# A hybrid decoder block on one core: the mixer in natural channel order, and a first and last expert pass with loads in halves

## The chip, the cores and the metric

The program runs on one core of one Trainium2 chip. The metric is the device time of one execution in microseconds, the median of several runs; lower is better. Everything is float32.

## What is computed

One decoder block over 256 tokens of 1024 channels: a pooling branch and a sliding-window attention branch, both gated, an output projection with a residual, then a top-4-of-32 mixture of experts with a residual, and a last RMSNorm. Cut to what matters here:

```python
h = rmsnorm(x, norm1_g)
u, q, k, v, g_pool, g_attn = split(h @ w_in)              # w_in 1024 x 3328
mixed = sigmoid(g_pool) * y_pool + sigmoid(g_attn) * y_attn
x = x + mixed @ w_out                                     # w_out 1024 x 1024
t = rmsnorm(x, norm2_g)
gates = softmax over the 4 largest of t @ w_router + b_router, 0 elsewhere
for e in range(32):                                       # w_up 1024 x 2048, w_down 1024 x 1024 each
    out += gates[:, e] * (clamped_swiglu(t @ w_up[e] + b_up[e]) @ w_down[e] + b_down[e])
return rmsnorm(x + out, final_g)
```

The experts' weights are 403 MB of the 430 MB that the program moves.

## The kernel before

**Ring of weights.** All large weights go through `ring`, ten slots of 2 MB (16 KB in each of the 128 partitions). SyncE (SP) issues the loads in one fixed order: 11 for the mixer, then 12 for each of 16 passes. A pass handles two experts, up to 64 chosen tokens of each. Its loads 0 to 7 are `w_up` in four steps `kk` of two experts each (two k rows to a slot, a k row being 128 of the 1024 input channels), loads 8 to 11 are `w_down` in two steps. `wait_freed` makes SP wait, before it issues a load, until TensorE is done with the load that lay in the same slot: semaphore `up_done` for `kk` 0 to 2, `cols_done` for `kk` 3, `down_done` for the two down steps. In pass 0, loads 0 to 9 wait for units of the mixer (`last_use`), load 8 for `w_out0_done`, load 9 for `outT3`; loads 10 and 11 wait for `kk` 0 of pass 0 itself (L309 issues them), and loads 0 and 1 of pass 1 for its `kk` 1.

**Mixer.** x is turned on TensorE (L592), normalized by DVE into `hT` (L981), and multiplied with the columns of `w_in` (L612, L623, L632). A channel of the model lies in partition p as k of `(p k)`, so the turned x and the output projection take every eighth column: `acc[:, t, k:D:KD]` at L592 and `w[:, k % 4, c:D:KD]` in `out_part` (L716). `out_part(c, k)` writes channel group c of the new x, turned; DVE adds the old x (L1082) into `x1T`. For each c TensorE then runs `logits_part`: the router's matmuls (L731), and sums of squares as matmuls of the ACT's squares (L511) with a column of ones (L735). `turn_back` (L742) turns `x1T` back; ACT and DVE copy it twice, scaled into `x1r` (L520) and plain into `acc` (L523, L1187).

**Routing and passes.** ACT takes the root (L513), DVE computes logits, the four chosen experts and ranks (L1087 to L1113) around three small matmuls (L770 to L772), and builds the 0/1 matrix `pick`. `gather` (L782) fetches a pass's tokens out of `x1r`, DVE copies them to `xgT` with the norm's weight (L1139). `pe_pass` runs the `up` matmuls (L827, 16 for each `kk`; TensorE takes each as two instructions), then `turn_hid` (L820) turns each half of the activated result for the `down` matmuls (L878), and four matmuls (L914) scatter the result back; DVE adds them to `acc` (L1144). The activation of chunk j of four is DVE's L1168, L1169, L1171, the ACT's sigmoid L547, DVE's product L1174, on one set of buffers. Pass 0 also holds `up_bias`, a second gather, two turns and `down_bias`.

**The end.** In pass 15 the last two loads are split by columns into six smaller ones (L318, semaphores `tail_landed`). ACT squares `acc` in four pieces of 512 columns (L567), takes two roots (L573), DVE scales and stores are issued by SP in three pieces (L1255, L382, L385).

Queues: SP issues all weights and the stores, ACT's queue the small inputs, POOL's queue two transfers of the attention bias. Each engine runs its own instructions in the order of the program.

```python
ins = nc.tensor.matmul(...)                 # up, kk < 3: all j for k, then the next k
ins.then_inc(up_done, 1)                    # once per kk
for j in range(NJ):                         # kk == 3: both k for j, then the next j
    for k in (2 * kk, 2 * kk + 1):
        ins = up(k, j, w)
    ins.then_inc(cols_done, 1)
```

## Time and profile before

| what | value |
|---|---|
| median of 3 runs | 1114.65 us (1114.25, 1114.65, 1119.39) |
| the profiled execution, its own time | 1119.8 us |
| its span, first to last instruction | 1118.0 us |
| TensorE (PE) busy | 1033.2 us, 92% |
| DVE, ACT, POOL busy | 250.0, 104.9, 8.3 us |
| DMA | 429.99 MB, 385 GB/s over the span |
| mean granted TensorE clock | 0.978 of full speed |

The profile's page gives busy times of each engine (PEld is TensorE's weight load, beside its matmuls), the span in 40 slices, the chain of waits that ended last, groups of instructions by line and tile, and the DMA issues. A matmul's busy time is partly modelled, so the distance between starts says more than the duration of one. SPq and ACTq rows are DMA issues of those engines.

### The profile page before, as it was taken

The page shows a single profiled execution, that of the slowest core. Times are in us where ns is not written, and L with a number is a line of the kernel's source. Part 1 is how long each engine was busy: PE and PEld are TensorE (multiplying, and loading weights), DVE is VectorE, ACT ScalarE, POOL GpSimd, SP SyncE. Part 2 cuts the span into 40 slices and gives each one's busy share as a digit, 9 for nine tenths or more (in the row PEclk, how much of TensorE's full clock was granted, in tenths as well). Part 3 has the DMA queues.
Part 4 walks back from the last instruction along what each step waited for, and adds up shares of the span by engine and source line. Part 5 has one row for each costly group of instructions (what it writes and reads, how often), then busy time and mean ns, then how long its engine had stood idle before and what let it go on. Part 6 is the DMA issues. An engine that isn't in the chain of part 4 may idle for free.

```text
span 1118.0 us, 11365 instructions
## 1 busy us (share of the span) xinstructions
PE 1033.2 (92%) x4930; PEld 504.1 (45%) x4930; DVE 250.0 (22%) x562; ACT 104.9 (9%) x238; POOL 8.3 (1%) x20
## 2 busy tenths in 40 slices
PE   7999998999999998989898989898989899898987
PEld 6888897343333434333333424242424243333322
DVE  2332113322121212121212213030212121212122
ACT  2131013000000000000000000010100000000002
POOL 1100000000000000000000000000000000000000
PEclk9999998999999999999999999999999999999998
DMA  9703982899999999999999999999999999999993
GB/s 335 293 1 136 427 376 81 357 429 427 427 429 427 426 429 427 427 429 426 428 429 427 428 429 428 427 428 427 428 428 427 428 426 429 427 427 429 428 414 135
DMA packets 42367, 429.99 MB, mean 385 GB/s; under 512 B 4771, under 2 KB 6604, under 8 KB 17996
## 3 DMA queue, kind: packets, MB, share of 16 engines
q1 hardware_dynamic: 39952, 427.57, 91.0%
q0 software_dynamic: 304, 1.06, 0.3%
q10 hardware_dynamic: 2060, 0.61, 0.3%
q8 instruction: 41, 0.67, 0.2%
q14 instruction: 10, 0.08, 0.0%
HBM read 428.16 MB, written 1.06 MB: 384 GB/s over the span
## 4 chain that ended last, share of the span: by engine, by line
PE 54%; DMA 44%; issue 0%; SPq 0%; DVE 0%; ACT 0%; DVEq 0%; ACTq 0%
DMA ring<-in_w_down 39%; PE bank L827 17%; PE bank L878 14%; PE bank L612 9%; PE bank L914 4%; DMA ring<-in_w_up 4%; PE bank L716 3%; PE bank L782 2%; PE bank L623 1%; PE bank L811 1%; DMA ring<-in_w_in 1%; PE bank L820 1%; SPq L309 0%; PE bank L632 0%; PE bank L735 0%
## 5 line engine op out<-in xcount | busy, mean ns | idle before, releaser
L827 PE MATMUL bank<-ring,z_buf 128*64 128x512 f32 x2048 | 468.8, 612 | 50.0 <-issue 27.7
L827 PEld LDWEIGHTS bank<-ring,z_buf 128*64 128x64 f32 x2048 | 156.7, 141 | 347.2 <-issue 347.2
L878 PE MATMUL bank<-ring,h_buf 128*64 128x512 f32 x1024 | 228.5, 598 | 10.6 <-DMA ring<-in_w_down 10.0
L878 PEld LDWEIGHTS bank<-ring,h_buf 128*64 128x64 f32 x1024 | 80.4, 137 | 136.0 <-issue 133.9
L1168 DVE TENSOR_SCALAR swi<-bank 128x256 f32<-128x256 f32 x64 | 27.2, 425 | 310.0 <-PE bank L827 304.9
L612 PE MATMUL bank<-h_buf,ring 128*128 128x256 f32 x336 | 75.7, 380 | 0.0
L612 PEld LDWEIGHTS bank<-h_buf,ring 128*128 128x128 f32 x336 | 63.5, 190 | 8.8 <-issue 0.2
L782 PE MATMUL bank<-u_buf,m_buf 128*128 128x128 f32 x512 | 63.5, 278 | 0.5 <-DVE u_buf L1123 0.5
L547 ACT ACTIVATE swi<-swi 128x256 f32<-128x256 f32 x64 | 26.7, 417 | 387.1 <-DVE swi L1168 387.1
L782 PEld LDWEIGHTS bank<-u_buf,m_buf 128*128 128x128 f32 x512 | 60.9, 195 | 1.3 <-issue 1.3
L914 PE MATMUL bank<-y,u_buf 128*128 128x512 f32 x128 | 59.2, 605 | 0.0
L1139 DVE TENSOR_TENSOR z_buf<-bank,g2x 128x512 f32<-128x512 f32 x32 | 22.1, 692 | 158.6 <-PE bank L782 158.6
L1144 DVE TENSOR_TENSOR acc<-acc,bank 128x512 f32<-128x512 f32 x64 | 44.0, 687 | 30.1 <-PE bank L914 30.1
L914 PEld LDWEIGHTS bank<-y,u_buf 128*128 128x128 f32 x128 | 23.0, 189 | 35.2 <-issue 35.2
L1179 DVE COPY y<-bank 128x512 f32<-128x512 f32 x16 | 11.1, 692 | 116.1 <-PE bank L878 116.1
L716 PE MATMUL bank<-m_buf,ring 128*128 128x256 f32 x128 | 32.8, 411 | 0.0
L538 ACT COPY h_buf<-bank 128x512 f32<-128x512 f32 x32 | 18.5, 577 | 145.9 <-PE bank L820 145.9
L716 PEld LDWEIGHTS bank<-m_buf,ring 128*128 128x128 f32 x128 | 31.1, 335 | 0.0
L820 PEld LDWEIGHTS bank<-ident,h_buf 128*128 128x128 f32 x128 | 17.8, 209 | 26.0 <-issue 26.0
L534 ACT COPY u_buf<-bank 128x256 f32<-128x256 f32 x16 | 6.0, 373 | 242.8 <-PE bank L790 242.8
L1174 DVE TENSOR_TENSOR h_buf<-swi 128x256 f32<-128x256 f32 x64 | 27.2, 425 | 2.5
L1171 DVE SCALAR_TENSOR_TENSOR swi<-swi 128x256 f32<-128x256 f32 x64 | 27.2, 425 | 2.2
(176 smaller groups left out, 374.0 us busy)
## 6 DMA issues: line engine op xcount, KB each, us to landing
ring<-in_w_up SPq DMA_DIRECT2D x128, 2048.0 KB, 36.8
ring<-in_w_down SPq DMA_DIRECT2D x62, 2048.0 KB, 36.8
ring<-in_w_in SPq DMA_DIRECT2D x6, 2048.0 KB, 18.3
ring<-in_w_out SPq DMA_DIRECT2D x2, 2048.0 KB, 16.5
ring<-in_w_pool_proj SPq DMA_DIRECT2D x1, 2048.0 KB, 24.5
ring<-in_w_attn_proj SPq DMA_DIRECT2D x1, 2048.0 KB, 22.3
ring<-in_w_down SPq DMA_DIRECT2D x2, 1024.0 KB, 32.1
ring<-in_w_down SPq DMA_DIRECT2D x4, 512.0 KB, 11.0
```

Of the source, the lines that this page charges most:

```text
L547: nc.scalar.activation(sig, glu, ACT.Sigmoid, scale=ALPHA).then_inc(sigmoid_ready, 1)
L612: ins = nc.tensor.matmul(dst, w[:, k, c * P:(c + 1) * P], rhs[:, k, :], start=(k == 0), stop=(k == kn - 1))
L716: return nc.tensor.matmul(outs[c % 4][:, (c // 4) * SEQ:(c // 4 + 1) * SEQ], w[:, k % 4, c:D:KD], mixedT[:, k, :], start=(k == 0 and c < 4 ...
L782: ins = nc.tensor.matmul(b[:, k * P:(k + 1) * P], x1r[:, t, (4 * half + k) * P:(4 * half + k + 1) * P], pick[:, t, :], start=(t == 0), sto ...
L820: ins = nc.tensor.transpose(turn_bank[:, c * P:(c + 1) * P], hid[:, m * CH + c:(m + 1) * CH:4], ident[:, :])
L827: ins = nc.tensor.matmul(up_banks[j][e * SLOTS:(e + 1) * SLOTS, :], xgT[:, k, e * SLOTS:(e + 1) * SLOTS], w[e].rearrange("p (k n) -> p k n ...
L878: ins = nc.tensor.matmul(down_banks[n][e * SLOTS:(e + 1) * SLOTS, :], hidT[:, k, e * SLOTS:(e + 1) * SLOTS], w[e], start=(k == 0), stop=(k ...
L914: nc.tensor.matmul(scatter_banks[q][:, :], spreadT[:, t * P:(t + 1) * P], y[:, n * CH:(n + 1) * CH], start=True, stop=True).then_inc(scatt ...
L1144: nc.vector.tensor_tensor(acc[:, t, n * CH:(n + 1) * CH], acc[:, t, n * CH:(n + 1) * CH], scatter_banks[q][:, :], ALU.add).then_inc(added, 1)
L1168: nc.vector.tensor_scalar(glu, pairs[:, :, 0], LIMIT, None, ALU.min).then_inc(glu_ready, 1)
L1171: nc.vector.scalar_tensor_tensor(lin, lin, 1.0, glu, ALU.add, ALU.mult).then_inc(gated_ready, 1)
L1174: nc.vector.tensor_tensor(hid[:, j * CF:(j + 1) * CF], lin, sig, ALU.mult).then_inc(hid_ready, 1)
```

## The change

In words:

- **Channel order.** `w_in`, `w_router` and the norm weights are loaded with `(k p)` instead of `(p k)`, so channel k * 128 + p lies in partition p. The transposes of x (L592) and the weights of `out_part` (L716) become contiguous. `norm1_g` in that order is a load of 1024 single elements; so is a second load of `norm2_g` (`g2`); `w_router` becomes 1024 pieces of 128 B. The experts keep `(p k)`; `turn_back` is now a matmul with a permuted identity (`deal`) instead of a transpose, and ACT's copy writes `x1r` in the experts' order.
- **Squares.** DVE adds the squares of groups 0 to 6 into `sq_sum`; TensorE sums only `sq_sum` and the last group, in a bank of its own and ahead of the last logits.
- **Copies to `acc`.** The plain copies of ACT and DVE (L523, L1187) are gone; POOL writes `acc` from `x1r` and `std`.
- **`keep_warm`.** Matmuls of the identity whose result is not used: 7 before the ranks, 2 before and 3 behind the first gather, 4 and 5 in the last pass.
- **First pass.** Loads 10 and 11 come in halves: the first when k row 0 of `kk` 0 is done (`rows_freed`), the second when row 1 is done.
- **Last pass.** Loads 6 to 9 come in halves with semaphores of their own; `kk` 3 runs k row by k row; both `turn_hid` stand ahead of the down matmuls; the activation uses two sets of buffers, and POOL does the product; two scatter matmuls stand between the last down matmuls, and the copy of the second half of `y` and its two scatters go in halves of 256 columns (the copy in every pass).
- **The end.** POOL multiplies columns 0 to 511 with `final_g`, ACT scales and stores them; DVE does columns 512 to 1023, which SP stores.

```diff
-                             w_in_d[:, c * CH:c * CH + wide].rearrange("(p k) n -> p k n", p=P)).then_inc(full[n % R], LANDED)
+                             w_in_d[:, c * CH:c * CH + wide].rearrange("(k p) n -> p k n", p=P)).then_inc(full[n % R], LANDED)
...
+                if g == FIRST:
+                    for h in range(2):
+                        sp.wait_ge((rows_freed, up_done)[h], 1)
+                        for load in (LOADS - 2, LOADS - 1):
+                            load_half(slot_of(load), g, load, h, early_landed[h])
+                if g == LAST:
+                    for load, landed in ((UP_LOADS - 2, last_up_landed), (UP_LOADS, last_down_landed)):
+                        for e in range(2):
+                            wait_freed(g, load + e)
+                        for h in range(2):
+                            for e in range(2):
+                                load_half(slot_of(g * LOADS + load + e), g, load + e, h, landed[h])
...
+            for t in range(TT):
+                pool.wait_ge(*emptied_at("back3"))
+                nc.gpsimd.tensor_scalar(acc[:, t, :].rearrange("p (q k) -> p k q", k=KD), x1r[:, t, :].rearrange("p (k q) -> p k q", k=KD),
+                                        std[:, t:t + 1], None, ALU.mult).then_inc(x1_ready, 1)
+            for j in range(NJ):
+                glu, lin, sig = gate_bufs(j, True)
+                pool.wait_ge(gated_ready, LAST * NJ + (j + 1))
+                pool.wait_ge(sigmoid_ready, LAST * NJ + (j + 1))
+                nc.gpsimd.tensor_tensor(hid[:, j * CF:(j + 1) * CF], lin, sig, ALU.mult).then_inc(hid_ready, 1)
...
-            act.dma_start(g1x, norm1_g[0].rearrange("(p k) -> p k", p=P)).then_inc(g1x_loaded, 16)
+            act.dma_start(g1, norm1_g[0].rearrange("(k p) -> p k", p=P), allow_slow_non_contiguous=True).then_inc(g1_loaded, 16)
...
+            for t in range(TT):
+                act.wait_ge(rstd_ready, 2 * TT + t + 1)
+                act.wait_ge(scaled_ready, t + 1)
+                nc.scalar.activation(result[:, t, 0:CH], result[:, t, 0:CH], ACT.Copy, scale=rstd[:, t:t + 1]).then_inc(result0_ready, 1)
...
-                return nc.tensor.matmul(outs[c % 4][:, (c // 4) * SEQ:(c // 4 + 1) * SEQ], w[:, k % 4, c:D:KD], mixedT[:, k, :],
+                return nc.tensor.matmul(outs[c % 4][:, (c // 4) * SEQ:(c // 4 + 1) * SEQ], w[:, k % 4, c * P:(c + 1) * P], mixedT[:, k, :],
...
+            def squares_part(src, first):
+                for t in range(TT):
+                    ins = nc.tensor.matmul(square_bank[:, t:t + 1], src[:, t, :], ones[:, 0:1],
+                                           start=(first and t == 0), stop=not first, skip_group_check=True)
+                return ins
...
+            def keep_warm(b, n):
+                for _ in range(n):
+                    nc.tensor.matmul(b[:, 0:P], ident[:, :], ident[:, :], start=True, stop=True)
...
+                            if first and kk == 0:
+                                ins.then_inc((rows_freed, up_done)[k], 1)
...
+                    elif split:
+                        for k in (2 * kk, 2 * kk + 1):
+                            pe.wait_ge(last_up_landed[k % 2], 32)
+                            for j in range(NJ):
+                                ins = up(k, j, w)
+                                if k == KD - 1:
+                                    ins.then_inc(cols_done, 1)
```

TensorE between the mixer's last group and the first pass, as it stood (L731 router, L735 squares, L742 turns back, L770 ranks, L782 gather, L827 pass 0):

```order
L731 MATMUL bank<-rt_buf,h_buf 128x32 [waits x1T_ready]
L731 MATMUL bank<-rt_buf,h_buf 128x32
L735 MATMUL bank<-row_buf,swi 128x1 [waits x1sq_ready]
L735 MATMUL bank<-row_buf,swi 128x1
L742 MATMUL bank<-ident,h_buf 128x128
L742 MATMUL bank<-ident,h_buf 128x128 [waits emptied_by_dve]
L770 MATMUL bank<-swi,row_buf 128x32 [waits x1T_ready,chosen_ready,consts]
L782 MATMUL bank<-u_buf,m_buf 128x128 [waits pick_ready,x1r_ready]
L782 MATMUL bank<-u_buf,m_buf 128x128 x7
```

and as it stands now (L804 router, L810 squares, L817 turns back, L824 `keep_warm`, L856 ranks, L868 gather):

```order
L810 MATMUL bank<-row_buf,swi 128x1 [waits x1sq_added,emptied_by_dve]
L817 MATMUL bank<-u_buf,h_buf 128x128 [waits deal_ready]
L810 MATMUL bank<-row_buf,swi 128x1 [waits x1sq_ready]
L804 MATMUL bank<-rt_buf,h_buf 128x32 [waits x1T_ready]
L804 MATMUL bank<-rt_buf,h_buf 128x32
L817 MATMUL bank<-u_buf,h_buf 128x128 x2
L824 MATMUL bank<-ident 128x128 [waits x1T_ready]
L824 MATMUL bank<-ident 128x128 x6
L856 MATMUL bank<-swi,row_buf 128x32 [waits x1T_ready,chosen_ready,consts]
L868 MATMUL bank<-u_buf,m_buf 128x128 [waits pick_ready]
```

The squares moved ahead of the last logits, and seven unused matmuls stand between the turns and the ranks.

SP's loads of the first pass after the mixer's, now (before, the four L341 rows were one row of two L309 loads that waited for `up_done`):

```order
L329 DMA ring<-in_w_down 128x4096 [waits unit_done]
L341 DMA ring<-in_w_down 128x2048 [waits rows_freed]
L341 DMA ring<-in_w_down 128x2048
L341 DMA ring<-in_w_down 128x2048 [waits up_done]
L341 DMA ring<-in_w_down 128x2048
L325 DMA ring<-in_w_up 128x4096 [waits up_done] x4
```

The first half moved ahead of the second k row; the loads of pass 1 behind them wait for what they waited for.

TensorE in the last pass, now (L913 up, L906 turns, L982 down, L1010 scatter):

```order
L913 MATMUL bank<-ring,z_buf 64x512 [waits last_up0_landed]
L913 MATMUL bank<-ring,z_buf 64x512 [waits last_up1_landed]
L906 MATMUL bank<-ident,h_buf 128x128 [waits hid_ready]
L824 MATMUL bank<-ident 128x128 x5
L906 MATMUL bank<-ident,h_buf 128x128 [waits hidT_copied,hid_ready]
L982 MATMUL bank<-ring,h_buf 64x512 [waits last_down0_landed,hidT_copied,spreadT_copied]
L982 MATMUL bank<-ring,h_buf 64x512 [waits tail1_landed]
L1010 MATMUL bank<-y,u_buf 128x512 [waits y0_copied]
L982 MATMUL bank<-ring,h_buf 64x512 [waits tail2_landed]
L1010 MATMUL bank<-y,u_buf 128x256 [waits y1_copied] x2
L1010 MATMUL bank<-y,u_buf 128x256 x2
```

The second turn moved ahead of the down matmuls, and two scatters ahead of the last of them.

## Rows read from the trace of the kernel before

**Rows 1.** Page, part 2: GB/s of the DMA in 40 slices of 27.95 us.
```profile
GB/s 335 293 1 136 427 376 81 357 429 427 427 429 427 426 429 427 427 429 426 428 429 427 428 429 428 427 428 427 428 428 427 428 426 429 427 427 429 428 414 135
```

**Rows 2.** Windows: PE, PEld, DVE, ACT, POOL busy us; PEclk, DMA share, GB/s.
```profile
190.00:195.00 5.00, 5.00 (x20) 1.74 (x18) 0.30 (x1) 0.18 (x1) 0.00 (x0) 0.73 0.02 3
...
1090.00:1095.00 5.00, 5.00 (x18) 1.86 (x16) 0.00 (x0) 0.00 (x0) 0.00 (x0) 0.66 0.98 361
```

**Rows 3.** SP's timeline of DMA issues, first pass: start us, us, line, count.
```profile
156.94 41.78 SPq L309 DMA_DIRECT2D ring<-in_w_down  x4
208.43 25.61 SPq L305 DMA_DIRECT2D ring<-in_w_up  x8
```

**Rows 4.** Chain of waits in order of time, end of the mixer: start us, us.
```profile
99.94 41.64 PE bank L612 x192
141.57 19.09 PE bank L716 x80
160.67 0.36 PE bank L731 x4
161.03 0.42 PE bank L735 x4
161.45 2.12 PE bank L716 x8
...
180.06 1.48 PE bank L742 x13
```

**Rows 5.** Page, part 5: groups of three lines, busy us and mean ns.
```profile
L1168 DVE TENSOR_SCALAR swi<-bank 128x256 f32<-128x256 f32 x64 | 27.2, 425 | 310.0 <-PE bank L827 304.9
...
L612 PEld LDWEIGHTS bank<-h_buf,ring 128*128 128x128 f32 x336 | 63.5, 190 | 8.8 <-issue 0.2
...
L716 PEld LDWEIGHTS bank<-m_buf,ring 128*128 128x128 f32 x128 | 31.1, 335 | 0.0
```

**Rows 6.** PE's timeline, routing and first pass: start us, us, instructions, idle before.
```profile
183.21 0.38 PE L770 MATMUL bank<-swi,row_buf 128*128 128x32 f32 x2 [1.66 <-issue]
...
184.97 2.98 PE L782 MATMUL bank<-u_buf,m_buf 128*128 128x128 f32 x16 [0.49 <-DVE u_buf L1123]
189.01 8.88 PE L827 MATMUL bank<-ring,z_buf 128*64 128x512 f32 x32 [1.06 <-DVE z_buf L1139]
```

**Rows 7.** Start: DMA issue with us to landing, ACT's queue, DVE, PE; one DMA queue at 21:22.
```profile
small<-in_norm_g ACTq DMA_DIRECT2D x1, 4.0 KB, 4.6
...
1.89 0.37 ACTq L433 DMA_DIRECT2D small<-in_norm_g  x1
...
9.15 3.22 DVE L981 SCALAR_TENSOR_TENSOR h_buf<-ring,small,bank 128x256 f32<-128x256 f32 x8 [0.73 <-PE bank L600]
...
11.80 15.72 PE L623 MATMUL bank<-h_buf,ring 128*128 128x256 f32 x64 [2.00 <-DMA ring<-in_w_in]
...
q10 hardware_dynamic: 185, 0.00, 10.4%
```

**Rows 8.** PE's timeline in the last pass.
```profile
1069.78 8.78 PE L827 MATMUL bank<-ring,z_buf 128*64 128x512 f32 x32 [2.36 <-issue]
1079.60 7.09 PE L827 MATMUL bank<-ring,z_buf 128*64 128x512 f32 x32 [1.04 <-DMA ring<-in_w_up]
...
1089.50 8.78 PE L878 MATMUL bank<-ring,h_buf 128*64 128x512 f32 x32 [2.13 <-DMA ring<-in_w_down]
...
1099.64 7.09 PE L878 MATMUL bank<-ring,h_buf 128*64 128x512 f32 x32 [0.68 <-ACT h_buf L538]
```

**Rows 9.** End: timelines of ACT, DVE, SP; POOL's at 28.34 us.
```profile
1103.34 0.59 ACT L551 COPY y<-bank 128x512 f32<-128x512 f32 x1 [3.75 <-PE bank L878]
...
1110.39 0.69 DVE L1144 TENSOR_TENSOR acc<-acc,bank 128x512 f32<-128x512 f32 x1 [0.17 <-PE bank L914]
...
1114.39 0.99 SPq L385 DMA_DIRECT2D out<-m_buf  x2
...
28.34 1.89 POOL L424 TENSOR_TENSOR ring<-u_buf 128x1024 f32<-128x1024 f32 x1 [8.63 <-DVE u_buf L998]
```

More of the change, by code:

```diff
@@ L57, with landed_loads @@
 ALL_LOADS = MIXER_LOADS + PASSES * LOADS
+FIRST, LAST = 0, PASSES - 1
+IN_PARTS = ([(FIRST, LOADS - 2), (FIRST, LOADS - 1)]
+            + [(LAST, load) for load in range(UP_LOADS - 2, LOADS)])
+def landed_loads(slot, n):
+    parts = [MIXER_LOADS + g * LOADS + i for g, i in IN_PARTS]
+    return sum(m % R == slot and m not in parts for m in range(n))
 UNITS = ([(f"xT{m}", "act") for m in range(4)]
@@ L269, in load_at, with gate_bufs @@
         def load_at(n):
-            return full[n % R], LANDED * (n // R + 1)
+            return full[n % R], LANDED * landed_loads(n % R, n + 1)
         up_banks, down_banks, turn_bank, gather_bank = bank[0:4], bank[4:6], bank[6], bank[7]
         scatter_banks = [bank[6], bank[7], bank[4], bank[5]]
-        def x1_columns(j):
-            t, half = j % 2, j // 2
-            return acc[:, t, :].rearrange("p (q k) -> p k q", k=KD)[:, 4 * half:4 * half + 4, :]
+        def gate_bufs(j, last):
+            at = y if j % 2 and last else swi
+            return [at[:, n * CF:(n + 1) * CF] for n in range(3)]
         def slot_of(load):
@@ L553, in _ @@
             for g in range(PASSES):
-                act_pass(g, first=(g == 0))
+                act_pass(g, first=(g == FIRST), last=(g == LAST))
             act.wait_ge(extra_ready, 1)
@@ L832, in pe_pass @@
                 for kk in range(KK):
-                    w = [slot_load(2 * kk + e) for e in range(2)]
+                    if split and kk == 2:
+                        keep_warm(gather_bank, 4)
+                    if split and kk == KK - 1:
+                        w = [ring[:, slot_of(g * LOADS + 2 * kk + e), :] for e in range(2)]
+                    else:
+                        w = [slot_load(2 * kk + e) for e in range(2)]
                     if kk % 2 == 0:
@@ L917, in _, with scatter @@
-            pe.wait_ge(x1r_ready, 4)
+                def scatter(q, parts=1):
+                    t, n = q % 2, q // 2
+                    for i in range(parts):
+                        part = slice(i * CH // parts, (i + 1) * CH // parts)
+                        if t == 0:
+                            pe.wait_ge(*((y0_copied, g + 1) if n == 0 else (y1_copied, 2 * g + (2 if parts == 1 else i + 1))))
+                        ins = nc.tensor.matmul(scatter_banks[q][:, part], spreadT[:, t * P:(t + 1) * P],
+                                               y[:, n * CH + part.start:n * CH + part.stop], start=True, stop=True)
+                    ins.then_inc(scatter_done, 1)
@@ L936, in slot_load @@
                         slot = extra_slots[load]
-                        landed = sum(n % R == slot for n in range(ALL_LOADS - 2))
+                        landed = landed_loads(slot, ALL_LOADS)
                         pe.wait_ge(full[slot], t * (LANDED * extra_slots.count(slot))
@@ L1177, in dve_pass, with copy_y1 @@
                     copy_xg(g + 1, 1, gather_bank)
-                dve.wait_ge(down_done, g * MH + MH)
-                nc.vector.tensor_copy(y[:, CH:2 * CH], down_banks[1][:, :]).then_inc(y1_copied, 1)
+                def copy_y1():
+                    dve.wait_ge(down_done, g * MH + MH)
+                    for i in range(2):
+                        part = slice(i * CF, (i + 1) * CF)
+                        nc.vector.tensor_copy(y[:, CH + part.start:CH + part.stop], down_banks[1][:, part]).then_inc(y1_copied, 1)
+                if not last:
+                    copy_y1()
                 for q in range(4):
+                    if last and q == 2:
+                        copy_y1()
                     dve.wait_ge(scatter_done, g * 4 + (q + 1))
```

245 lines of the change are left out of this document (154 added, 91 removed).

## The prediction

> **What bounds the kernel now.** I read the page's slices first. From slice 8 on the DMA moves 426 to 429 GB/s and never stops until the last two slices; before that it stands at 1, 136 and 81 GB/s in slices 2, 3 and 6 [rows 1]. So the program has three parts: a mixer in which the DMA waits for ring slots, a stream of expert weights that the DMA bounds (25.2 MB a pass, 58.8 us at 428 GB/s, of which TensorE's six steps of 7.1 us [rows 8] fill 42.5), and a tail behind the last loads. What moves the end is when the stream restarts for good, its rate, and the tail.
>
> SP's timeline tells when it restarts: four down loads are issued from 156.94 to 198.72 us, the last two of them behind `kk` 0 of pass 0 (189.01 and 8.88 [rows 6]); the next load goes at 208.43, after `kk` 1 [rows 3]. These two loads are 4.2 MB, 9.8 us at 428 GB/s, so the DMA is out of work just as the next is released. From 208.4 on slots come free faster than the DMA fills them: a step takes 7.1 us of matmuls [rows 8] and seldom more than 2.6 of small ones. The stream's end is thus set by the end of `kk` 1 of pass 0. Before it TensorE is busy without a break from 99.94 [rows 4].
>
> **The change, in the clock of the profiled execution before.**
>
> *Start, +0.7 us.* TensorE starts at 11.80, released by the first `w_in` load; DVE starts `hT` at 9.15 [rows 7]. `norm1_g` was issued at 1.89 and landed 4.6 us later, 6.5, in 128 pieces. Now it is 1024 pieces on the ACT's queue. The row of that queue at 21:22, where single elements of `pool_scale` moved beside 2 KB pieces, shows 185 of them per us [rows 7]: 896 more take 4.8 us, landing at 11.3. DVE then needs 0.4 to write the first k of `hT`, so TensorE starts near 12 and waits a little at cold clock: I take 0.7. Bounds: a gain of 0.5 if the `(k p)` pieces of `w_in` come at 428 instead of some 385 GB/s; a loss of 3 if the small pieces run at half that pace beside the 4 KB pieces of x. I take a value near the low end because x is through by 5 us.
>
> *Mixer's end, 6.6 us to the logits.* Contiguous weights: L612's weight loads take 190 ns, the strided ones of L716 335 [rows 5]. L716 is 64 matmuls, two instructions each: 19.09 + 6 x 2.12 = 31.8 us [rows 4]. L612 ran 96 in 41.64, 0.434 each [rows 4], so 64 cost 27.8: 4.0 saved. Squares: 8 x 0.42 [rows 4] become 2 x 0.42, 2.5 saved. DVE's sum costs TensorE nothing: two operations of 0.42 [rows 5] and one of ACT fit in a group's 2.1 us; without that cover TensorE would wait for `x1sq_added` before its first square. Two turns of 0.22 replace three short ones, nothing. Logits complete before at 180.06 [rows 4], now 173.4. If the stride were not the cause, 4.0 falls away.
>
> *Ranks, 5.1 us left.* They started 3.15 after the logits [rows 4, 6]. The root now starts 0.35 before the logits, so they could start at 176.2. But behind the logits stand 14 turns, now full matmuls of 0.22 (first gather: 8 in 2.98 cold, about 1.95 warm), and 7 unused ones of 0.22: 173.4 + 4.7 = 178.1, against 183.21 [rows 6]. The unused matmuls take back 1.9 us here. POOL's copies lie beside this; `acc` is not wanted until pass 0's bias near 200. `g2` and the small pieces of `w_router` land within the first 40 us, hidden by the gates.
>
> *Gather and `kk` 0, 2.8 us.* Gather 2.98, up 8.88 [rows 6]; the same up step warm is 7.09 [rows 8]. The granted clock at 190:195 is 0.73 [rows 2], a mix of 1.2 and 2.4 GHz, behind a stretch with idle gaps of 1.66, 0.49 and 1.06 [rows 6]. With unused matmuls in two of them I take full clock: 1.0 + 1.8. Bound below: nothing.
>
> *First pass in halves, 0.* Leaving the start's 0.7 out, `kk` 0 now begins at 182.9 (ranks at 178.1, 1.76 to the gather, 1.95, and 1.06 to the copy [rows 6]); the first half goes out at 186.5, the second at 190.0, both are through at 194.9. The loads of pass 1 still wait for `kk` 1, 10.5 us later, 200.5. The DMA begins 3.5 us sooner and then stands idle for 5.6 us where it stood for none. Only if `kk` 1 ended before 194.9 would the halves be worth anything.
>
> Stream restarts 5.1 + 2.8 - 0.7 = **7.2 us** earlier; pass bodies and rate are unchanged, so all of it reaches the end.
>
> *Tail, 4.2 us* (times less the shift). Last up loads landed at 1079.6, the pair before at 1069.8 [rows 8]. With warm clock `kk` 2 ends 1076.9 (before: 8.78), k row 6, landed 4.9 earlier, ends 1080.4, row 7 at 1084.0 instead of 1086.7. The first chunk is ready at 1081.3; DVE has three operations for a chunk, 1.3 us by 0.425 each [rows 5], and POOL's product costs 0.47 (1.89 for 1024 columns [rows 9]): `hid` done 1087.0. Turn and copy 1.3: down starts 1088.3 (before 1089.50 [rows 8]), 7.1 without the cold 8.78, then the second half at once at 1095.4 instead of 1099.64 [rows 8]. Six k-column steps 5.3, two scatters 1.8, two steps 1.8: 1104.3. Half copy 0.45 and scatters 1.8: 1106.5; last add starts 1106.6 against 1110.39 [rows 9], 3.8 earlier. From there it took 5.0 to the last issue's end, 1115.38 [rows 9]; now add 0.7, root 1.6 (two square pieces in the chain, not four), reciprocal 0.2, two ACT scalings 1.2 (0.59 each [rows 9]), two issues 1.0: 4.7. Sum 4.1, with the shorter queue on SP 4.2. Bounds 1.5 to 5.5. The tail's pieces must have landed by 1102.5; they did by 1098.
>
> A rule speaks against halves. The window 1090:1095, with 1 MB and 512 KB loads, still shows 361 GB/s [rows 2]. At that rate the eight late halves, 8.4 MB, take 23.2 instead of 19.6 us; only row 7's landing is on the path, some 0.9 later. The Trainium skill, "DMA: Bandwidth & Descriptors", section Bandwidth, measures 341 GB/s for a 1 MB transfer against 425 for 16 MB; by it the sum would lose about 1.7 us. I hold with the queue full of other loads and leave it out.
>
> **Sum.** -7.2 - 4.2 = -11.4: 1108.4 for an execution like the profiled 1119.8. That one stands 5.2 above the median; against 1114.65 it gives **1103.2 us**.
>
> **The rivals.**
>
> *TensorE stays cold and the tail is held by POOL (0.13).* Unused matmuls are short; gaps remain. Loses 2.8 at the gather and 1.7 in the last down: 6.9 gained, 1107.8. For it: 0.66 at 1090:1095 [rows 2] behind a gap of only 2.13 [rows 8]. Where POOL's product and DVE's operation with two SBUF inputs exclude each other, a chunk costs 1.3 + 0.47, `hid` comes 1.9 later; with a warm clock alone that gives 1105.1. The Trainium skill, "SBUF — State Buffer", section SBUF: two separate sides, states such a lock; no row here shows it.
>
> *Small pieces late (0.12).* `norm1_g` lands at 14: 3 us lost, 1105.5.
>
> *The restart does not carry through (0.10).* The stream's end is held by memory, not by its start; or the new order saves nothing. Only the tail remains: 1110.4, within 0.5%. Against it: the steady 426 to 429 GB/s.
>
> *Slower (0.03): natural order starves the first loads.* The 2 KB pieces of one partition now lie 1.7 MB apart. If `w_in` came at a quarter of the rate, the first load, 10.05 us now, takes 40: 30 us later, 1132. It turns the result slower by 0.5% from a loss of 17 us, a landing near 29 instead of 11.75. Against it: `w_out`, in the same order with 4 KB pieces, falls in the slice of 427 GB/s [rows 1].
>
> **How the numbers follow.** Forecast 0.62. About 0.5%, 5.6 us, is what a measurement of this kernel can tell from no change; the three runs already span 5.1. Faster: forecast and two rivals, 0.87, less a little for such a spread, 0.86. Same 0.11, slower 0.03. Range: low end with all bounds good (0.5 more at start, 1.3 in the tail, 1.9 if the unused matmuls cost nothing) 1099; high end the cold rival plus 2 of the late start, 1109.8.
>
> **What would show it.** SP's first load of pass 1 near 201 instead of 208.4, with the DMA idle some 5 us before it; L789 (the old L716) at 0.43 per matmul; ranks right behind unused matmuls; first up step 7.1; TensorE's first `w_in` matmul at 12 to 12.5. In the last pass no gap between the two down steps, and the last add some 11 us earlier. I am wrong if the steady rate drops below 426, if the first matmul starts beyond 14, or if the stream restarts early but TensorE's steps in the tail are no closer to the last landing.

## The result and the profile after

The changed kernel takes 1110.27 us (median of 6 runs, 1109.44 to 1111.0), the kernel before 1116.45 beside it (6 runs, 1114.25 to 1122.37): ratio 0.9931, 95% interval 0.9908 to 0.9955. It is faster, by over 0.5% (0.69%), as forecast; but the predicted 1103.2 is 7 us too low, and 1110.27 lies half a microsecond above the range's end of 1109.8. Taken as a gain, 11.4 us were forecast from the median of 1114.65, with 4.9 at the small end of the range, and 6.2 were measured beside 1116.45. The profiled execution after took 1109.44 us, span 1107.5, 10.5 less than the span before.

The page's slices of the changed kernel, against [rows 1]. Columns are the 40 slices, now 27.7 us each:

```profile
GB/s 326 308 1 107 423 417 141 368 429 428 427 428 427 427 428 428 428 427 428 425 430 427 426 427 430 428 426 428 427 427 430 428 427 427 429 427 429 426 418 194
```

The steady rate is about what it was, 425 to 430 GB/s; one slice shows 425, just under the 426 that the prediction had set as a sign of being wrong, and its neighbour 430. SP's timeline of the first pass, against [rows 3]:

```profile
188.42 4.24 SPq L341 DMA_DIRECT2D ring<-in_w_down  x4
202.37 0.80 SPq L325 DMA_DIRECT2D ring<-in_w_up  x2
```

The first load of pass 1 goes at 202.37 instead of 208.43, 6.1 us sooner where 7.2 were predicted. PE's timeline from the start to pass 0, against [rows 4, 6, 7] (start us, us, instructions, idle before them):

```profile
13.28 3.32 PE L696 MATMUL bank<-h_buf,ring 128*128 128x256 f32 x7 [2.83 <-DVE h_buf L1114]
...
142.80 17.43 PE L789 MATMUL bank<-m_buf,ring 128*128 128x256 f32 x80
160.06 0.53 PE L804 MATMUL bank<-rt_buf,h_buf 128*128 128x32 f32 x4
...
174.81 0.61 PE L804 MATMUL bank<-rt_buf,h_buf 128*128 128x32 f32 x4
175.25 3.37 PE L817 MATMUL bank<-u_buf,h_buf 128*128 128x128 f32 x28
178.46 1.73 PE L824 MATMUL bank<-ident 128*128 128x128 f32 x14
180.03 0.31 PE L856 MATMUL bank<-swi,row_buf 128*128 128x32 f32 x2
...
181.62 2.05 PE L868 MATMUL bank<-u_buf,m_buf 128*128 128x128 f32 x16
...
184.73 7.09 PE L913 MATMUL bank<-ring,z_buf 128*64 128x512 f32 x32 [0.39 <-DVE z_buf L1278]
```

The same timeline of the kernel before, at the ends of the output projection:

```profile
141.41 19.26 PE L716 MATMUL bank<-m_buf,ring 128*128 128x256 f32 x80
...
179.48 0.58 PE L735 MATMUL bank<-row_buf,swi 128*128 128x1 f32 x4
```

From the first row of the output projection, the logits (and, before, their squares) are complete after 32.6 us (174.81 + 0.61 - 142.80) instead of 38.65 (179.48 + 0.58 - 141.41), the ranks start 4.6 behind them instead of 3.15, and the first up step 4.70 behind the ranks instead of 5.80. The projection's weight loads go with most of the first figure (groups by line: busy us, mean ns, idle us), against [rows 5]:

```profile
L789 PEld LDWEIGHTS bank<-m_buf,ring 128*128 128x128 f32 x128 | 23.9, 190 | 3.0
```

335 ns became 190, the same as L612's contiguous loads in [rows 5]. The last pass, PE's timeline, against [rows 8]:

```profile
1062.30 13.95 PE L913 MATMUL bank<-ring,z_buf 128*64 128x512 f32 x64 [1.09 <-issue]
1076.91 0.75 PE L906 MATMUL bank<-ident,h_buf 128*128 128x128 f32 x4 [0.66 <-POOL h_buf L484]
1077.50 1.28 PE L824 MATMUL bank<-ident 128*128 128x128 f32 x10
1079.16 0.75 PE L906 MATMUL bank<-ident,h_buf 128*128 128x128 f32 x4 [0.38 <-POOL h_buf L484]
1080.67 12.35 PE L982 MATMUL bank<-ring,h_buf 128*64 128x512 f32 x56 [0.77 <-ACT h_buf L604]
```

Two steps of up run as one block and the down matmuls as another, at full clock. The end, timelines of ACT, SP, ACT's queue, and the stores' summary, against [rows 9]:

```profile
1099.23 0.63 ACT L634 ACTIVATE h_buf<-acc 128x512 f32<-128x512 f32 x1 [2.15 <-DVE acc L1283]
...
1101.36 1.21 SPq L432 DMA_DIRECT2D out<-m_buf  x2
...
1101.86 0.98 ACTq L648 DMA_DIRECT2D out<-m_buf  x2
...
DMA to landing us min/median/max: 2.5/2.9/4.6
```

From the last issue's end, 1102.84, it is 4.66 us to the end of the span; before it was 2.6.

### The profile page after: what moved, and what is told of

Read it like the earlier page. It is cut to its first block, busy times and chain, and to the rows that moved or that the text cites. A ratio compares the mean times of both kernels' runs of the same rounds, so it can differ in the third digit from the quotient of the medians.

```text
span 1107.5 us, 11484 instructions
## 1 busy us (share of the span) xinstructions
PE 1029.6 (93%) x4968; PEld 499.7 (45%) x4968; DVE 252.0 (23%) x578; ACT 104.6 (9%) x238; POOL 21.5 (2%) x28
## 4 chain that ended last, share of the span: by engine, by line
PE 57%; DMA 41%; DVE 1%; issue 0%; SPq 0%; ACT 0%; ACTq 0%; POOL 0%; POOLq 0%; DVEq 0%
DMA ring<-in_w_down 29%; PE bank L913 19%; PE bank L982 15%; DMA ring<-in_w_up 11%; PE bank L685 9%; PE bank L1010 4%; PE bank L789 3%; PE bank L868 2%; PE bank L696 1%; PE bank L897 1%; DMA small<-in_norm_g 1%; PE bank L906 1%; PE bank L817 0%; PE bank L705 0%; PE bank L824 0%
## 5 line engine op out<-in xcount | busy, mean ns | idle before, releaser
L913 PE MATMUL bank<-ring,z_buf 128*64 128x512 f32 x2048 | 467.0, 611 | 45.9 <-issue 25.3
L913 PEld LDWEIGHTS bank<-ring,z_buf 128*64 128x64 f32 x2048 | 156.5, 140 | 340.6 <-issue 340.4
L982 PE MATMUL bank<-ring,h_buf 128*64 128x512 f32 x1024 | 226.9, 595 | 7.4 <-DMA ring<-in_w_down 6.6
L982 PEld LDWEIGHTS bank<-ring,h_buf 128*64 128x64 f32 x1024 | 78.7, 137 | 133.1 <-issue 130.6
L1309 DVE TENSOR_SCALAR swi<-bank 128x256 f32<-128x256 f32 x62 | 26.3, 425 | 309.7 <-PE bank L913 304.8
L868 PE MATMUL bank<-u_buf,m_buf 128*128 128x128 f32 x512 | 62.6, 275 | 0.0
L868 PEld LDWEIGHTS bank<-u_buf,m_buf 128*128 128x128 f32 x512 | 60.0, 193 | 0.8 <-issue 0.8
L1010 PE MATMUL bank<-y,u_buf 128*128 128x512 f32 (+1 forms) x132 | 59.5, 593 | 0.5 <-DVE y L1325 0.5
L1283 DVE TENSOR_TENSOR acc<-acc,bank 128x512 f32<-128x512 f32 x64 | 44.1, 689 | 45.2 <-PE bank L1010 45.2
L1010 PEld LDWEIGHTS bank<-y,u_buf 128*128 128x128 f32 x132 | 23.7, 189 | 35.8 <-issue 34.2
L1325 DVE COPY y<-bank 128x256 f32<-128x256 f32 x32 | 12.1, 420 | 98.7 <-PE bank L982 98.7
L906 PEld LDWEIGHTS bank<-ident,h_buf 128*128 128x128 f32 x128 | 17.8, 208 | 26.5 <-issue 24.3
L789 PE MATMUL bank<-m_buf,ring 128*128 128x256 f32 x128 | 29.3, 383 | 0.0
L1310 DVE TENSOR_SCALAR swi<-bank 128x256 f32<-128x256 f32 x62 | 25.7, 415 | 0.0
## 6 DMA issues: line engine op xcount, KB each, us to landing
ring<-in_w_up SPq DMA_DIRECT2D x126, 2048.0 KB, 36.8
ring<-in_w_down SPq DMA_DIRECT2D x58, 2048.0 KB, 36.8
```

Source lines behind the costliest of these rows:

```text
L789: return nc.tensor.matmul(outs[c % 4][:, (c // 4) * SEQ:(c // 4 + 1) * SEQ], w[:, k % 4, c * P:(c + 1) * P], mixedT[:, k, :], start=(k == ...
L868: ins = nc.tensor.matmul(b[:, k * P:(k + 1) * P], x1r[:, t, (4 * half + k) * P:(4 * half + k + 1) * P], pick[:, t, :], start=(t == 0), sto ...
L906: ins = nc.tensor.transpose(turn_bank[:, c * P:(c + 1) * P], hid[:, m * CH + c:(m + 1) * CH:4], ident[:, :])
L913: ins = nc.tensor.matmul(up_banks[j][e * SLOTS:(e + 1) * SLOTS, :], xgT[:, k, e * SLOTS:(e + 1) * SLOTS], w[e].rearrange("p (k n) -> p k n ...
L982: ins = nc.tensor.matmul(down_banks[n][e * SLOTS:(e + 1) * SLOTS, :], hidT[:, k, e * SLOTS:(e + 1) * SLOTS], w[e], start=(k == 0), stop=(k ...
L1010: ins = nc.tensor.matmul(scatter_banks[q][:, part], spreadT[:, t * P:(t + 1) * P], y[:, n * CH + part.start:n * CH + part.stop], start=Tru ...
```

## Four cuts through the span

Each span was divided at the same four points: the end of the first 64 matmul instructions of `w_in` (two to a matmul; "the first 64 matmuls" below), the first load of pass 1, the start of `kk` 2 in the last pass, and the end. Profiled executions, us:

| run | first matmul | end of first 64 | to first load of pass 1 | to `kk` 2 of last pass | to the end |
|---|---|---|---|---|---|
| before | 11.80 | 27.52 | 180.91 | 861.35 | 48.2 |
| before_again | 11.89 | 25.97 | 180.91 | 860.8 | 48.1 |
| after | 13.28 | 28.90 | 173.47 | 859.93 | 45.2 |
| after_again | 13.31 | 29.99 | 173.47 | 860.03 | 45.0 |
| mixer_only | 13.22 | 28.74 | 173.46 | 861.0 | 46.6 |
| whole_first_again | 13.24 | 30.24 | 173.46 | 861.01 | 44.9 |
| no_warm_ranks | 13.20 | 28.94 | 172.72 | 860.07 | 45.5 |
| g_rows | 11.49 | 28.45 | 173.47 | 860.17 | 45.1 |
| both_gains | 11.57 | 25.65 | 172.73 | 860.02 | 45.3 |
| no_warm_last | 13.29 | 29.82 | 173.46 | 860.12 | 47.8 |

Of the columns with numbers, the third repeats to 0.01 us for the same code, so what differs there is the code's; the second doesn't, and of these four stretches it differs most between two executions of one kernel (1.55 us for the kernel before, 1.1 for the changed one).

## Experiments

**before_again** is the kernel before, unedited, once more.

> The kernel before, a second profiled execution. Theory A: the profiled execution of before (1119.8 us) was a long one of its kind, and the length lies behind the last loads or in the stream; then this one, if its own time is near 1114.5, has the same times up to 208.4 us (end of kk 1 of pass 0) within 0.3 us and is some 4 us shorter between there and the end. Theory B: executions differ at the start, by when x and the first weights land; then the first w_in matmul, at 11.80 us, moves by as much as the time does.

1117.58 us, span 1115.8: 2.2 under the first profiled execution. 1.55 of it lies before the end of the first 64 matmuls (which took 14.08 us instead of 15.72), 0.55 in the stream. The first matmul itself came at 11.89, so theory B is out, and theory A asked for an execution near 1114.5, which this was not. Twenty more executions beside it had a median of 1115.87. So the prediction's base execution was a long one.

**mixer_only** keeps the natural order, the sums of squares, POOL's copy and the unused matmuls at the gather; both passes, the activation and the end are as before.

```diff
-IN_PARTS = ([(FIRST, LOADS - 2), (FIRST, LOADS - 1)]
-            + [(LAST, load) for load in range(UP_LOADS - 2, LOADS)])
+IN_PARTS = ([(LAST, load) for load in range(LOADS - 2, LOADS)])
...
-act_pass(g, first=(g == FIRST), last=(g == LAST))
+act_pass(g, first=(g == FIRST))
```

> The mixer's part of the change alone (natural order, squares, POOL's copies to acc, unused matmuls around the first gather), with the passes and the end as before. Theory A, the two parts add: first load of pass 1 issued at 202.4 us as in the changed kernel, 6.0 before, and the time 5.5 to 6.5 us below before, with the last pass worth the remaining 1 to 3. Theory B, the tail holds the end by itself: the time falls by less than 3 us, and the last pass carries the gain.

1112.19 us, 0.9956 (0.9939 to 0.9972) of the kernel before, in medians 3.7 faster; the table has it 7.45 sooner from the first 64 matmuls to the stream's restart, like the whole change. Neither theory's time came (5.5 to 6.5 faster, or less than 3). In its own profile the tail is 46.6 and not 48.2 because its first down step came at full clock, 7.09 us, which the two profiles of before do not show ([rows 8]: 8.78, behind an equal wait). Its `kk` 2 was cold as there:

```profile
1063.23 8.78 PE L884 MATMUL bank<-ring,z_buf 128*64 128x512 f32 x32 [2.36 <-issue]
...
1082.96 7.09 PE L935 MATMUL bank<-ring,h_buf 128*64 128x512 f32 x32 [2.12 <-DMA ring<-in_w_down]
```

So 1.6 us of the tail's gain against these two profiles can come without any edit in the last pass.

**whole_first** takes only the first pass's halves away, and ran in two sessions.

```diff
-                if g == FIRST:
-                    for h in range(2):
-                        sp.wait_ge((rows_freed, up_done)[h], 1)
-                        for load in (LOADS - 2, LOADS - 1):
-                            load_half(slot_of(load), g, load, h, early_landed[h])
...
```

> The changed kernel with loads 10 and 11 of pass 0 whole again, issued at the end of kk 0. Theory A, the halves are worth nothing because the next load waits for kk 1 anyway: first load of pass 1 at 202.4 us as with halves, time within 0.7 us of the changed kernel. Theory B, they carry the DMA ahead: 3.5 us slower without them. Theory C, the idle stretch that they leave costs a new start of the DMA: 1 to 1.5 us faster without them.

> The first pass's last two loads whole again, behind all of kk 0, once more beside the changed kernel in one session. Theory from the traces so far (from the first load of pass 1 to the start of kk 2 in the last pass 860.95 us without the halves, 859.93 with them): 0.6 to 1.2 us slower than the changed kernel. The prediction's own term was 0: then within 0.3.

1111.37 us (0.995, 0.9931 to 0.9968) and 1111.3 (0.9953, 0.9938 to 0.9968), the second beside a changed kernel of 1110.6: 0.7 slower, with intervals that overlap. The traces say 1.0, all of it in the fourth column of the table. Windows of PE (busy us, PEclk, DMA share, GB/s) show how. With halves, the changed kernel:

```profile
198.00:200.00 2.00, 2.00 (x12) 1.00 0.93 393
200.00:202.00 2.00, 2.00 (x12) 1.00 0.01 4
202.00:204.00 2.00, 2.00 (x16) 1.00 0.52 123
```

and without them, whole_first:

```profile
200.00:202.00 2.00, 2.00 (x12) 1.00 0.95 410
202.00:204.00 2.00, 2.00 (x18) 1.00 1.01 434
204.00:206.00 2.00, 2.00 (x10) 1.00 0.85 287
```

With halves the queue is empty when pass 1's first load is issued; without them loads 10 and 11 are still under way then, and what is left of them comes out of the stream that bounds the rest. The prediction gave the halves nothing because it set the loads' 9.8 us against 10.5 us of waiting. It left out the start of a transfer into an empty queue: whole_first issues loads 10 and 11 at 192.84, and its windows show 90 GB/s from 192 to 194, 197 from 194 to 196 and 442 only from 196 on.

Beside mixer_only, measured in the same session, whole_first differs by the last pass and the end alone: 1111.37 against 1112.19, 0.8 us in medians.

**no_warm_ranks** takes away the seven unused matmuls before the ranks.

```diff
-            keep_warm(begin("ranks"), 7)
```

> The changed kernel without the seven unused matmuls ahead of the ranks. Theory A, they only delay: ranks 1.5 us earlier than 180.03, gather and first up step as short as now (1.9 and 7.1 us), time 1.5 us shorter. Theory B, they hold the clock: ranks 1.5 us earlier, but the first gather takes near 3.0 and the first up step up to 8.9 us, granted clock near 0.75 between 186 and 192 us, and the time is 0 to 1.3 us longer.

1109.09 us (1108.96 to 1109.83; 0.9929, 0.9904 to 0.9953). By the table they cost 0.75 us on the path and not the 1.9 that the prediction charged, since without them the gather waits 0.70 for DVE's `pick`. And in this profile they keep nothing warm: the first up step takes 7.09 without them too. It starts at 184.02 here, 184.73 in the changed kernel.

**g_rows** loads both norm weights as 16 rows of 512 bytes and turns them on TensorE.

```diff
-            act.dma_start(g1, norm1_g[0].rearrange("(k p) -> p k", p=P), allow_slow_non_contiguous=True).then_inc(g1_loaded, 16)
+            act.dma_start(g_rows[0:KD, :], norm1_g[0].rearrange("(k p) -> k p", p=P)).then_inc(g_loaded, 16)
+            act.dma_start(g_rows[KD:2 * KD, :], norm2_g[0].rearrange("(k p) -> k p", p=P)).then_inc(g_loaded, 16)
...
+            nc.tensor.transpose(bank[7][:, 0:2 * KD], g_rows[:, :], ident[0:2 * KD, 0:2 * KD]).then_inc(g_turned, 1)
```

> The changed kernel with both norm weights loaded as eight rows of 512 B each, turned by one TensorE transpose and copied by DVE, in place of 1024 single elements each. Theory A, the late start is the single elements of norm1_g: hT begins near 9.8 us instead of 12.66, the first w_in matmul near 12 instead of 13.28, released by the w_in load, and the time is 1.3 us shorter. Theory B, the first w_in load itself comes later in the new order: hT begins early but the first matmul stays at 13.0 or later, and the time stays.

1108.71 us (1108.0 to 1109.61; 0.9922, 0.9904 to 0.994). DVE's wait in the changed kernel, its timeline at the start:

```profile
12.66 2.44 DVE L1114 SCALAR_TENSOR_TENSOR h_buf<-ring,small,bank 128x256 f32<-128x256 f32 x6 [4.13 <-DMA small<-in_norm_g]
```

and PE's timeline in g_rows:

```profile
8.42 0.28 PE L672 MATMUL bank<-ident,g_rows 16*128 16x16 f32 x1
...
11.49 5.06 PE L700 MATMUL bank<-h_buf,ring 128*128 128x256 f32 x11 [0.26 <-DMA ring<-in_w_in]
```

The first matmul waits for `w_in` again and comes 1.8 us sooner, which is the gain of the medians too (1.6 and 1.9 against the changed kernel's two). So the small pieces cost 1.8 us of start here, and a turn of 0.28 avoids them.

**stores_sp** gives all four stores to SP; **end_old** has the old end in it, the scaling on DVE alone and three stores from SP.

```diff
-            for t in range(TT):
-                act.wait_ge(result0_ready, t + 1)
-                act.dma_start(out_d[t][:, 0:CH], result[:, t, 0:CH]).then_inc(stored, 16)
...
```

```diff
-                act.wait_ge(scaled_ready, t + 1)
-                nc.scalar.activation(result[:, t, 0:CH], result[:, t, 0:CH], ACT.Copy, scale=rstd[:, t:t + 1]).then_inc(result0_ready, 1)
...
+            sp.wait_ge(result1_ready, 1)
+            sp.dma_start(out_d[0], result[:, 0, :]).then_inc(stored, 16)
...
```

> The changed kernel with all four stores issued by SP, each when its piece is ready. Theory A, the ACT's queue is what lands late (4.6 us from issue against 2.5 to 3.1 on SP): last landing 2.6 us after the last issue, 1.5 to 2 us shorter. Theory B, the four stores, 1 MB, end when their bytes are through, some 2.8 us behind the first, whatever queue they are in: within 0.5 us of the changed kernel.

> The changed kernel with the end as before (DVE scales all, SP stores three pieces, no POOL or ACT in it). Theory A, the new end gives back what it gains, since its stores are issued together and land 4.6 us after: the last add to the end takes 7.6 as before against 8.1, within 0.7 us of the changed kernel. Theory B, the new end is worth the 1.1 us by which DVE's part is shorter: 1 us slower without it.

1110.23 us (1109.88 to 1111.18) and 1110.77 (1109.83 to 1111.02), against 1110.27 and 1110.6 of the changed kernel: no difference. SP's timeline in end_old:

```profile
1103.35 0.36 SPq L431 DMA_DIRECT2D out<-m_buf  x1
1104.21 1.91 SPq L434 DMA_DIRECT2D out<-m_buf  x2
```

From the first square after the last add to the last issue's end it is 5.4 us in end_old (1100.68 to 1106.12) and 3.6 in the changed kernel; from the same point to the end of the span, 8.32 and 8.27. What the new end wins in issuing, the stores take back in landing. Windows of all engines at the end of the changed kernel (the last two columns are DMA share and GB/s):

```profile
1102.00:1103.00 1.00, 0.00 (x0) 0.00 (x0) 0.20 (x1) 0.44 (x1) 0.00 (x0) 0.50 0.79 289
1103.00:1104.00 1.00, 0.00 (x0) 0.00 (x0) 0.00 (x0) 0.00 (x0) 0.00 (x0) 0.50 1.05 385
1104.00:1105.00 1.00, 0.00 (x0) 0.00 (x0) 0.00 (x0) 0.00 (x0) 0.00 (x0) 0.50 0.95 350
1105.00:1106.00 1.00, 0.00 (x0) 0.00 (x0) 0.00 (x0) 0.00 (x0) 0.00 (x0) 0.50 0.07 27
```

and of the kernel before:

```profile
1116.00:1117.00 1.00, 0.00 (x0) 0.00 (x0) 0.00 (x0) 0.00 (x0) 0.00 (x0) 0.50 1.00 389
1117.00:1118.00 1.00, 0.00 (x0) 0.00 (x0) 0.00 (x0) 0.00 (x0) 0.00 (x0) 0.50 0.08 27
```

The four stores go out within 1.5 us and nearly all of their 1 MB has moved by 1105; the span ends 2.5 us later, where before it ended 1.0 behind the last busy window. So the bytes alone don't explain the end, and what holds it stays open. end_old is not quite the old end either: from the last add's start its span runs 8.2 us (1100.83 to 1109.0), where before and in mixer_only it was 7.6, and its last store took 1.25 us to issue.

**no_warm_last** takes away the unused matmuls of the last pass.

```diff
-                    if split and kk == 2:
-                        keep_warm(gather_bank, 4)
...
-                    keep_warm(gather_bank, 5)
```

> The changed kernel without the nine unused matmuls of the last pass. Theory A, they hold the clock: without them kk 2 or the first down step takes 8.8 instead of 7.1 us in some runs or all, 1.5 to 3 us slower, and the runs spread more. Theory B, they do nothing: the waits there are short enough now, same steps, same time within 0.5 us.

1111.47 us (1110.68 to 1114.25; 0.9951, 0.9931 to 0.997), 0.9 to 1.2 above the changed kernel in medians. Its profiled execution took 1113.19, one of its two long ones; there the tail is 47.8, 2.6 longer:

```profile
1063.40 13.95 PE L913 MATMUL bank<-ring,z_buf 128*64 128x512 f32 x64 [2.38 <-issue]
...
1080.26 1.13 PE L906 MATMUL bank<-ident,h_buf 128*128 128x128 f32 x4 [1.50 <-POOL h_buf L484]
1082.16 14.47 PE L979 MATMUL bank<-ring,h_buf 128*64 128x512 f32 x56 [0.77 <-ACT h_buf L604]
```

The turn takes 1.13 instead of 0.75 and the down matmuls 14.47 instead of 12.35. PE's window there (busy us, PEclk, DMA share, GB/s):

```profile
1082.00:1090.00 8.00, 7.84 (x26) 0.71 0.97 360
```

0.71 is a mix of 1.2 and 2.4 GHz, behind a stretch in which TensorE stood idle between turns. So the five between the turns earn their place, by up to 2.5 us, in an execution like this one; the other four of its six runs lie within 1.1 us of 1110.6. The four before `kk` 2 are not shown to do anything: without them `kk` 2 and 3 took 13.95 as with them, behind an idle stretch of 2.38 us, though the kernel before and mixer_only had a cold `kk` 2 of 8.78 behind one of 2.36.

**hid_dve** puts the last pass's product back on DVE.

```diff
-                    if last:
-                        continue
...
```

> The last pass's products for hid on VectorE again, behind its three operations for each chunk, instead of GpSimd. Theory A (GpSimd works beside VectorE without a price, the chunks are paced by VectorE's three operations, 1.13 us each, and GpSimd's 0.73 counts only once, behind the last): with a fourth operation of about 0.42 a chunk takes some 1.5, hid is done 0.7 to 0.9 us later, and the kernel is 0.7 to 0.9 us slower than the changed kernel. Theory B, the lock of the prediction's rival (a GpSimd product and a VectorE operation with two SBUF inputs exclude each other): then VectorE's third operation, 0.42 now, is shorter here, and the run is no slower or faster.

1112.42 us (1110.32 to 1113.28; 0.996, 0.9946 to 0.9974) beside 1110.6. From the start of `kk` 2 to the down matmuls it takes 19.41 us instead of 18.37. DVE's timeline of a chunk, in the changed kernel, with POOL's product behind it:

```profile
1074.85 0.42 DVE L1309 TENSOR_SCALAR y<-bank 128x256 f32<-128x256 f32 x1
1075.18 0.41 DVE L1310 TENSOR_SCALAR y<-bank 128x256 f32<-128x256 f32 x1
1075.63 0.42 DVE L1312 SCALAR_TENSOR_TENSOR y<-y 128x256 f32<-128x256 f32 x1
...
1075.01 0.73 POOL L484 TENSOR_TENSOR h_buf<-swi 128x256 f32<-128x256 f32 x1 [887.95 <-DVE swi L1312]
```

and in hid_dve:

```profile
1076.30 0.42 DVE L1306 SCALAR_TENSOR_TENSOR y<-y 128x256 f32<-128x256 f32 x1
1076.76 0.43 DVE L1309 TENSOR_TENSOR h_buf<-y 128x256 f32<-128x256 f32 x1
```

DVE's operation with two SBUF inputs takes 0.42 beside POOL's product and without it, so theory A holds for the stage: a chunk goes from 1.13 to 1.59 us, and the stage is 1.0 longer. The median is 1.8 above the changed kernel's, though: four of its seven runs took 1112.4 to 1113.3, the profiled one 1110.62, and no profile exists of a long one, so the rest stays open. The product and that operation overlap by only 0.1 us in the changed kernel; a lock between the two is not seen here, and not excluded by more than that.

**after_again** is the changed kernel once more, and **both_gains** joins g_rows and no_warm_ranks; both in one session.

> The changed kernel itself once more, beside the three kernels of this call and the kernel before, so that small differences between versions are read on one chip in one session. 1110.3 us median (1109.4 to 1111.0 in its first six executions), 0.993 of the kernel before. Every theory expects the same; a median away from 1110.3 by more than 0.7 us would say how far two sessions may be compared.

> Two pieces that each gained alone, put together: norm weights loaded as 16 rows of 512 bytes and turned on TensorE, and no unused matmuls before the ranks. Theory: they are on the path at different places (TensorE's first w_in matmul 1.8 us sooner; ranks about 1.1 us sooner, the clock staying full) and both before the first load of pass 1, so they add: first load of pass 1 near 200.8, 1.5 to 2.5 us under the changed kernel of this call, near 1107.8. Rival, the later parts take it back (the cold phase of TensorE at the start is longer when it begins sooner, or the clock falls at the gather without the unused matmuls): then no better than the better of the two alone, 1108.7 to 1109.1.

The changed kernel repeats at 1110.6 us (1110.37 to 1110.9; 0.9946, 0.9931 to 0.996). both_gains takes 1107.25 (1105.58 to 1107.75; 0.9916, 0.9902 to 0.9931): 3.3 under it, the best of all. By the table the unused matmuls give 0.75 and the first matmul 1.7; 0.9 us remain without a cause shown. The profile is of its fastest execution, 1105.58, whose first 64 matmuls took 14.08 us, 2.6 less than in after_again; how long they took in its other runs, 1107.17 and above, no profile shows (the last section).

## Why the prediction was right, and where it was wrong

The direction and the mechanism held: the restart of the stream bounds the end, and what is saved before it reaches the end undiminished (the fourth column, 859.93 to 861.35 us in all profiles). The size did not. That 1110.27 is also the number of the rival "the restart does not carry through", 1110.4, is a coincidence: the restart came 6.1 us sooner and was carried through. Two pairs of profiles, by the prediction's own terms (us gained; the first pair is the one profiled at first, the second before_again and after_again):

| term | predicted | first pair | second pair |
|---|---|---|---|
| start, to the end of the first 64 matmuls | -0.7 | -1.4 | -4.0 |
| mixer's end, ranks, gather and `kk` 0 | 7.9 | 7.4 | 7.4 |
| stream, with the first pass in halves | 0 | 1.4 | 0.8 |
| tail | 4.2 | 3.0 | 3.1 |
| sum | 11.4 | 10.5 | 7.3 |

- **Start, the term furthest off in the second pair (3.3 us), not in the first (0.7).** The pace of the small pieces, 185 per us, was near: `norm_g` landed 10.7 us after its issue, at 12.6 where 11.3 was predicted, and the first matmul came at 13.28, where 12 to 12.5 was given. "Waits a little at cold clock" priced the wait and not what follows it. While DVE waited 4.13 us for the weights, TensorE stood idle 2.83, and the first 64 matmuls then took 15.5 to 17.0 us in all ten profiles with the small pieces; without them they took 14.08 in two of four (before_again, both_gains), 15.72 in the other profile of before and 16.96 in g_rows. That the longer wait makes the slow case the rule is suggested by these counts, not shown. The second pair has both halves of this: 1.4 from the later first matmul, 2.6 from its pace. The rival "small pieces late" had the right place and, by luck, about the right size, 3 us: it had the pieces land at 14, and they landed at 12.6.
- **Mixer's end.** 6.0 of 6.6. The stride's share came as predicted: 40 matmuls took 17.26 us, 0.43 each, and 19.09 before. No run has the order without the squares, so the two are told apart by this spacing only. Of what is missing, 0.4 lies in the six groups of four matmuls behind them, which took 1.81 us from start to start (160.43 to 162.24) where 0.434 each would give 1.74, and 0.2 in the last group, where squares and turns stand between the projection and the last logits.
- **Ranks.** 1.5 lost, as predicted (the sum's 6.6 less 5.1). The share of the unused matmuls was wrong inside it, 0.75 and not 1.9.
- **Gather and `kk` 0.** 1.1 and 1.8, 2.9 against 2.8; the gather went from 2.98 to 2.05 and the step from 8.88 to 7.09. But the unused matmuls of the ranks were not what did it, as no_warm_ranks shows; which of those around the gather are needed was not tried.
- **First pass in halves.** Nothing predicted, 1.0 measured, for the reason given with whole_first. The prediction's sum was off as well: halves issued from 186.5 that need 9.8 us are through at 196.3 and not at 194.9. Measured, they were issued from 188.42 and through at 200, and the DMA stood idle for some 3 us, not 5.6.
- **Tail.** From the start of `kk` 2 to the last add 37.07 us, predicted 36.8; before it was 40.61. That term was 3.5 of 3.8. POOL's product took 0.73 and not 0.47, and counts once. The failed piece is the end: the last issue's end did come sooner, 3.5 us behind the last add's start against a predicted 4.7, but the prediction took the time from there to the end as unchanged, 2.6, and it became 4.66. Of the end's new layout nothing is left. And of the 3.0 that the tail gained, 1.6 is the clock of one down step, which mixer_only had without the last pass's edits: beside it, in medians, whole_first gained 0.8 with the last pass and the end together, where 4.2 was predicted.
- **The rule on small transfers.** PE's windows of the last pass show the DMA with halves in the queue:

```profile
1063.00:1070.00 7.00, 7.00 (x34) 1.00 1.01 422
1070.00:1077.00 7.00, 6.34 (x31) 1.00 1.00 411
1077.00:1082.00 5.00, 3.85 (x25) 1.00 1.03 402
```

 mixer_only, which runs the same stage at the same time with whole loads until the last pieces, had 424, 426 and 373 GB/s in these windows. The Trainium skill, "DMA: Bandwidth & Descriptors", section Bandwidth, has 341 GB/s for one transfer of 1 MB; with the queue full the halves kept 402 to 422 and lost at most 4% to whole loads, and TensorE waited for none of them. The sum was right to leave it out. (The prediction's 1.7 us at 341 GB/s does not follow from its 0.9 at 361: the same 2.1 MB at 341 against 428 gives an estimate of 1.3.)
- **From one execution to a median.** The 11.4 was worked out against an execution of 1119.8 us and taken from a median of 1114.65. The clock and the length of the first 64 matmuls differ between executions of one kernel, so gains that consist of cold clock made warm are probably largest against the longest execution. The median of the kernel before over six runs was 1116.45, which is 1.8 of the 7 us; the start's 3.3 (second pair), the tail's 1.1 and the mixer's 0.5, less 0.8 from the halves, are another 4.1. Some 1.2 us are left. No profile exists of an execution of the kernel before near 1114.3 us, so how it differs from the two shown stays open.

## What to carry to other kernels

When a stream bounds most of a kernel, measure each version from cut to cut (here the stream's restart and the last landing), because medians hide a small loss beside a large gain: here a load in single elements took back 1.8 us, and a turn on TensorE costs 0.28. Where a wait is added in front of TensorE, price the clock of the matmuls behind it too, and fill an idle stretch with unused matmuls only where a profile shows that the work behind it runs cold. A gain worked out inside one profiled execution is not to be taken from the median of others without asking which of its parts differ between executions.

## What the runs showed of the hardware

- **The same first matmuls take different lengths.** The 64 matmul instructions of L696 (L623, L700 elsewhere) took 14.08 us in before_again and both_gains, 15.5 to 17.0 elsewhere. PE's windows in g_rows and then both_gains, the same code at this place (busy us, count of matmuls, PEclk, DMA share, GB/s):

```profile
14.00:15.00 1.00, 1.00 (x3) 1.00 1.08 365
...
18.00:19.00 1.00, 1.00 (x6) 1.00 1.08 382
```

```profile
14.00:15.00 1.00, 1.00 (x6) 1.00 1.08 364
```

 In g_rows three or four matmuls start in each microsecond until 17 us, which is the pace of 1.2 GHz, and six from 18 us on; in both_gains it is six from the start. The granted clock reads 1.00 throughout in both. It reads 0.50 in the kernel before at 12 to 15 us, where the pace is also three or four. So at the very start of g_rows the clock row can't be trusted, and the count of matmuls shows the pace. The Trainium skill, "TensorE: Matmul & The Clock Gate", section Part 1: The HAM clock gate (the "warmup" mystery), says that the number of cold matmuls at the start varies from run to run and that this is under 1% of a typical span. The runs agree, 2.9 us of 1107; but that is almost half of this change's gain.
- **Long executions of the kernel before tend to show a lower mean clock.** In the last session the three under 1115.6 us had 0.981 to 0.984 and the longest, 1119.72, had 0.976; between them it is mixed (1117.27 at 0.983), and beside before_again one of 1121.72 had 0.982. So the clock is not all of it. The changed kernel's six in the last session lay within 0.6 us, at 0.982 to 0.984. The changed kernel is steadier, for a reason that no run here isolates.
- **One idle stretch, two clocks.** Behind 2.36 us without a matmul `kk` 2 of the last pass ran cold in before and mixer_only (8.78 us), behind 2.38 it ran at full clock in no_warm_last; behind 2.1 us the first down step took 8.78 in before and 7.09 in mixer_only. A gap of this length can go either way, and a single profile doesn't price it.
- **An empty queue's first store lands in 2.5 us; the last of four issued within 1.5 us in 4.6.** Issuing them sooner or from two queues changed nothing in the time.
